# Two-block layer on one core: GpSimd's copy of the tokens moved behind the first product granule, and the rows of w_out split in the order of the features

## The chip, the cores and the metric

One Trainium2 chip, one core. The metric is the device time of one execution in microseconds, the median of several runs. The engines are TensorE (PE in the rows, PEld for its weight loads), VectorE (DVE), ScalarE (ACT), GpSimd (POOL) and SyncE (SP), which issues the DMAs.

## The reference, cut to what matters

256 tokens of 1024 features pass two blocks. The first is a hybrid mixer and then a mixture of 32 experts; the second is an LRU and gated-attention mixer and a dense feed-forward part. The change touches the entry and the end of the first mixer:

```
def first_block(x, ...):
    h = x
    hn = rmsnorm(h, norm_mix[i])
    h = h + hybrid_mixer(hn, w_in[i], ..., w_out[i])      # w_out: 2048 x 1024
    hn = rmsnorm(h, norm_ffn[i])
    h = h + hierarchical_moe(hn, ...)
    return rmsnorm(h, final_norm)

# the end of hybrid_mixer
    return jnp.concatenate([ssd_out, sc_out], axis=-1) @ w_out
```

`ssd_out` and `sc_out` are normed and carry a gain per feature (`ssd_norm`, `sc_norm`).

## The kernel before, in words

All matrices are fp32. A product is done in three fp32r passes: every weight is split into a high part (`w_hi`, rounded to fp32r) and the rest (`w_lo`), and so is every activation. Weights come in units of 2 MB, one of six slots of the buffer `ring` each; a unit is cut into four granules of 128 x 1024 elements. For granule g, ScalarE runs `hi(g)` (L583 without a gain, L585 with one), VectorE runs `lo(g)` (L593, or L595 with a gain), and TensorE multiplies. `w_hi` and `w_lo` hold two granules each, so `hi(g)` waits until TensorE has finished granule g-2 (it counts `gran_used`), `lo(g)` waits for `hi(g)`, and TensorE's granule g waits for both. Each engine's order is written out by hand, as one loop over g in which other steps are placed at fixed g.

**Opening.** The tokens land in `x_tok`. ScalarE squares block 0, VectorE block 1, GpSimd takes the power (L505). Then VectorE scales block 0 into `xdt` (L500) and ScalarE block 1 (L487); both are wanted by TensorE's 16 transposes (L515). `turn_act` and `turn_dve` (L534, L540) split the transposed tokens into `act_p`, and granule 0 follows (L613). From g = 2 on VectorE does one short convolution per granule behind `lo(g)` (`conv_xbc`, L1433, three steps with both inputs in SBUF). GpSimd, behind L505, copies `x_tok` to `res` (L912, two copies of 128 x 1024), makes two masks and `blk64` (L900 to L919), and then raises `const_ready` to 2. ScalarE waits for that before it overwrites `x_tok` (`keep_x(0)`, L1080, at g = 5).

**Order of features.** The residual `res` is kept in an order that makes later transposes give rows p of 8 features each: position c*128 + q of a row holds feature q*8 + c. `natural(b)` reads or writes `res` in the order of the features, which steps 128 elements (512 bytes) from one element to the next; `in_eights` of a bank has that order in one contiguous run.

**Output product.** `w_out` is units 11 to 14, granules 44 to 59 (G_WO = 44, GA = 60). Each of its granules is one row chunk of 128 x 1024, split with a gain (L585, L595), and TensorE adds 12 matmuls of 512 columns (`row_gran`, L664) to four banks. Behind the last granule `add_res` adds the four banks to `res` (L682), and TensorE transposes `res` for the router (L2200). The second block's mixer ends with `add_halves` (L691), where bank and `res` are both contiguous.

After the router come 32 experts, whose weights (6 MB each) stream from HBM.

Of the kernel before, what the change touches and what calls it, by code (L numbers as in the profile page):

```python
# [25 lines left out]
ALU = mybir.AluOpType  # L26
# [5 lines left out]
TB = T // P  # L32
D = 1024
KC = D // P
# [21 lines left out]
GR = 1024  # L56
# [19 lines left out]
def bcast(ap, shape):  # L76
    return ap.broadcast_to(shape)


def two_block_layer(nc, x, w, out):  # L80

    with ExitStack() as ctx:
        build(nc, ctx, x, w, out)


def build(nc, ctx, x, w, out):
    def sb(name, shape, dt=F32, where=ctx):
        return where.enter_context(nc.sbuf_tensor(name, shape, dt))

    def sem(name):  # L90
        return ctx.enter_context(nc.semaphore(name))
# [13 lines left out]
    res = sb("res", [P, TB, D])  # L105
# [25 lines left out]
    x_tok = sb("x_tok", [P, TB, D], where=ph)  # L131
# [60 lines left out]
    grans = []  # L192

    def whole(u):
        return ring[:, u % SLOTS, :]

    def cols_unit(wt, *spans):

        u = len(units)
        parts, at = [], 0  # L200
        for c0, n in spans:
            dst = whole(u).rearrange("p (k n) -> p k n", k=KC)[:, :, at:at + n]
            rows = "(p k) n -> p k n" if wt is w["w_in_2"] else "(k p) n -> p k n"
            parts.append((dst, wt.rearrange(rows, p=P)[:, :, c0:c0 + n]))
            at += n
        units.append(parts)
        return u

    def rows_unit(wt, chunk, n):

        u = len(units)
        dst = whole(u)[:, 0:n * D].rearrange("p (k n) -> p k n", k=n)
        src = wt[chunk * P:(chunk + n) * P, :].rearrange("(k p) n -> p k n", p=P)
        units.append([(dst, src)])
        return u
# [9 lines left out]
        for k in range(0, KC, kn):  # L225
            grans.append((u, whole(u).rearrange("p (k n) -> p k n", k=KC)[:, k:k + kn, c0:c0 + n], None))

    def row_grans(u, gains):
        for j, gain in enumerate(gains):
            grans.append((u, whole(u)[:, j * GR:(j + 1) * GR], gain))  # L230

    def sc_raw(c0, c1):

# [2 lines left out]
    def pcol(name, i):  # L236
        return par[:, PCOLS[name] + i:PCOLS[name] + i + 1]
# [12 lines left out]
    for c in range(0, 16, 4):  # L250
        ks = MIX[c:c + 4]
        row_grans(rows_unit(w["w_out"], ks[0], 4),
                  [pcol("sc_norm", k - 8) if k >= 8 else pcol("ssd_norm", k) for k in ks])
    UA, GA = len(units), len(grans)
    G_Q, G_K, G_V, G_G, G_LG = GA + 4, GA + 6, GA + 8, GA + 12, GA + 16
    turn_grans(cols_unit(w["w_in_2"], (0, P), (P, 512 - P)), range(4))
    u = cols_unit(w["w_in_2"], (O_Q, 512))
# [6 lines left out]
    for c in (0, 4):  # L264
        row_grans(rows_unit(w["w_out_2"], c, 4), [None] * 4)
# [10 lines left out]
    def ffn_out(f0, n):  # L276
        row_grans(rows_unit(w["w_ffn_out_2"], f0, n), [None] * n)
        for i in range(n):
            GO[f0 + i] = len(grans) - n + i
# [17 lines left out]
    const_ready = sem("const_ready")  # L297
# [3 lines left out]
    gran_used = sem("gran_used")  # L301
# [45 lines left out]
    ssd_norm = sem("ssd_norm")  # L347
# [92 lines left out]

    neg_half = sm[:, 8:24]
    N_ROWS_A = sum(tile == 0 for _, tile, _, _ in PROWS)
    N_SMALL = len(PROWS) + 3 + 2 + 1 + NG + 1 + 2 + 3

# [13 lines left out]
    def natural(b, p0=0, p1=P):  # L458

        return res[:, b, :].rearrange("t (c p) -> t p c", c=KC)[:, p0:p1, :]  # L460
# [8 lines left out]
    def in_eights(row):  # L469
        return row.rearrange("t (p c) -> t p c", c=KC)  # L470
# [32 lines left out]
    def norm_pool(pool, n):  # L503
        pool.wait_ge(ms_ready, n + 1)
        nc.gpsimd.tensor_tensor(sm[:, 4:6], sm[:, 2:4], neg_half[:, 0:2], ALU.pow).then_inc(rstd_ready, 1)  # L505
# [165 lines left out]
    def piece_ready(dve, n, at, g):  # L671
        if at < 3:
            dve.wait_ge(bank_done, 3 * n + at + 1)
        else:
            dve.wait_ge(gran_used, g + 1)

    def add_res(dve, n, g, banks, done):

        for at, (b, half) in enumerate(BY_BLOCK):
            r = natural(b, 64 * half, 64 * half + 64)  # L680
            piece_ready(dve, n, at, g)
            ins = nc.vector.tensor_tensor(r, r, in_eights(banks[2 * b + half][:, :]), ALU.add)  # L682
            if half:
                ins.then_inc(done, 1)

# [36 lines left out]
    for g, (u, _, _) in enumerate(grans):  # L722
        last_gran[u] = g
# [173 lines left out]
    def _(pool):  # L897
        def mask(tile, op, step, mult, base=0):
            plain = tile.bitcast(F32)
            link_pool(pool, nc.gpsimd.memset(plain, 1.0))  # L900
            link_pool(pool, nc.gpsimd.affine_select(out=tile, in_=plain, compare_op=op, fill=0.0, base=base,
                                                    pattern=[[step, P]], channel_multiplier=mult))
# [5 lines left out]
                       allow_small_or_imprecise_dtypes=True)  # L908
        nc.gpsimd.memset(pad[:, :, 0:3], 0.0).then_inc(const_ready, 1)
        norm_pool(pool, 0)  # L910
        for b in range(TB):
            nc.gpsimd.tensor_copy(natural(b), in_eights(x_tok[:, b, :]))  # L912
        mask(m_le[:, :], ALU.is_ge, 1, -1)
        mask(m_gt[:, :], ALU.is_gt, -1, 1)
        link_pool(pool, nc.gpsimd.memset(blk64[:, :], 1.0))
# [1 line left out]
        link_pool(pool, nc.gpsimd.affine_select(out=v, in_=v, compare_op=ALU.is_ge, fill=0.0, base=0,  # L917
                                                pattern=[[-64, 2], [0, 64]], channel_multiplier=1))
        nc.gpsimd.affine_select(out=v, in_=v, compare_op=ALU.is_ge, fill=0.0, base=63,  # L919
                                pattern=[[64, 2], [0, 64]], channel_multiplier=-1).then_inc(const_ready, 1)  # L920


        pool.wait_ge(u_ready, 1)
# [37 lines left out]
        def by_head(tile, b):  # L961
            return tile[:, b, :].rearrange("p (h d) -> p h d", h=HEADS)
# [21 lines left out]
        for b in range(TB):  # L984
            ins = nc.gpsimd.tensor_tensor(by_head(xdt, b), by_head(x_tok, b),
                                          bcast(adt[:, 7, b, :].unsqueeze(2), [P, HEADS, HD]), ALU.mult)
        ins.then_inc(xdt_ready, 1)
        for it in range(9):
# [16 lines left out]
            if it == 7:  # L1005
# [18 lines left out]
                                pattern=[[1, P]], channel_multiplier=-1).then_inc(const_ready, 1)  # L1024
# [376 lines left out]
    def _(dve):  # L1401
# [142 lines left out]
        for g in range(GA):  # L1544
# [32 lines left out]
            for h in range(2):  # L1577
                for n in range(2 * h, 2 * h + 2):
# [4 lines left out]
                    if g == (G_WO + 1, G_WO + 3)[h]:  # L1583
                        lo_ssd(n)
        add_res(dve, 0, GA - 1, bank[0:4], res_mix)


# [945 lines left out]
```

## Time and profile before

| | |
|---|---|
| median of 3 runs | 955.83 us (955.31 to 957.48) |
| the profiled execution's own time | 955.47 us |
| its span | 953.7 us |
| TensorE busy | 782.6 us, 82% |
| VectorE busy | 465.6 us, 49% |
| ScalarE busy | 318.0 us, 33% |
| GpSimd busy | 99.0 us, 10% |
| DMA | 286.67 MB, mean 301 GB/s |

The span is the time between the first and the last instruction that the trace shows; the execution's own time has 1.8 us around it. Busy times of engines overlap. The expert stage (about 240 to 640 us) runs with all 16 DMA engines busy; ahead of and behind it TensorE is the engine that is nearly always busy.

### The profile page before, as it was taken

The numbers are of one execution on the slowest core, as the hardware profiler recorded it, in microseconds if no ns is written. First come the engines' busy times: TensorE is split into PE (matmuls) and PEld (weight loads), VectorE is DVE, ScalarE is ACT, GpSimd is POOL, SyncE is SP. The second block draws the span as 40 slices with busy tenths as digits, with TensorE's granted clock in tenths as the row PEclk, the third lists the DMA queues.
The fourth block names the chain that finished last, engine by engine and source line by source line (L and its number), as shares of the span: only waits on it lengthen the run. The fifth ranks groups of instructions, "written<-read, shape, count | busy, mean of one in ns | idle before, by whom it ended". The sixth has DMA issues, their size and how long they took to land.

```text
span 953.7 us, 15749 instructions
## 1 busy us (share of the span) xinstructions
PE 782.6 (82%) x6548; PEld 601.2 (63%) x6548; DVE 465.6 (49%) x815; ACT 318.0 (33%) x525; POOL 99.0 (10%) x116
## 2 busy tenths in 40 slices
PE   5999999999984764747646566479999999999997
PEld 5988999777643432334423333236888888888885
DVE  6865849547421121201302012024968776766776
ACT  5764346732100000000000000003597554444444
POOL 3019673300000000000000000000000100000000
PEclk9999999999997887777979798779999999999999
DMA  9895243677999999999999999999975455555101
GB/s 318 272 354 177 90 177 145 259 311 294 415 427 428 426 429 426 427 427 429 428 429 427 428 429 427 429 428 388 363 266 178 155 189 201 183 177 177 45 1 45
DMA packets 72534, 286.67 MB, mean 301 GB/s; under 512 B 11882, under 2 KB 38688, under 8 KB 59936
## 3 DMA queue, kind: packets, MB, share of 16 engines
q1 hardware_dynamic: 71876, 284.81, 75.9%
q10 hardware_dynamic: 604, 1.10, 0.3%
q8 instruction: 39, 0.64, 0.3%
q14 instruction: 15, 0.12, 0.0%
HBM read 284.85 MB, written 1.05 MB: 300 GB/s over the span
## 4 chain that ended last, share of the span: by engine, by line
PE 54%; DMA 28%; issue 8%; DVE 4%; POOL 3%; ACT 2%; SPq 1%; POOLq 0%; DVEq 0%; ACTq 0%
DMA pair_d<-in_w_up_dram 22%; PE bank L664 11%; PE bank L613 11%; PE bank L629 9%; PE bank L2264 5%; PE bank L626 4%; PE bank L2288 4%; PE bank L641 4%; DMA ring<-in_w_in_dram 3%; DMA down_b<-in_w_down_dram 3%; PE bank L2230 1%; PE bank L2238 1%; PE bank L2095 1%; POOL seg_r L946 1%; ACT w_hi L583 1%
## 5 line engine op out<-in xcount | busy, mean ns | idle before, releaser
L593 DVE TENSOR_TENSOR w_lo<-ring,w_hi 128x1024 fp32r<-128x1024 f32 x135 | 174.7, 1294 | 101.9 <-ACT w_hi L583 101.5
L583 ACT ACTIVATE w_hi<-ring 128x1024 fp32r<-128x1024 f32 x136 | 144.2, 1060 | 178.3 <-PE bank L629 64.1
L613 PE MATMUL bank<-act_p,w_hi 128*128 128x256 f32 x736 | 137.7, 288 | 3.1 <-issue 2.0
L1776 DVE COPY y_e<-bank 32x256 f32<-32x256 f32 x64 | 27.2, 424 | 222.5 <-PE bank L2288 222.1
L629 PE MATMUL bank<-act_p,w_hi 128*128 128x512 f32 x344 | 119.3, 397 | 0.0
L613 PEld LDWEIGHTS bank<-act_p,w_hi 128*128 128x128 f32 x736 | 115.3, 192 | 6.0 <-issue 3.9
L1226 ACT ACTIVATE y_e<-bank 32x256 f32<-32x256 f32 x64 | 23.9, 374 | 256.7 <-PE bank L2288 256.4
L613 PE MATMUL bank<-act_p,w_lo 128*128 128x256 f32 x368 | 104.3, 283 | 0.0
L2288 PE MATMUL bank<-down_b,h_t 128*32 128x256 f32 x480 | 40.3, 493 | 74.6 <-issue 64.1
L664 PE MATMUL bank<-w_hi,act_q 128*128 128x512 f32 x288 | 90.6, 396 | 1.4 <-issue 0.8
L2264 PE MATMUL bank<-ring,moe 128*32 128x256 f32 x1472 | 84.0, 380 | 7.1 <-DVE moe L1739 6.7
L626 PE MATMUL bank<-act_p,w_lo 128*128 128x256 f32 x344 | 89.5, 281 | 0.0
L2288 PEld LDWEIGHTS bank<-down_b,h_t 128*32 128x32 f32 x480 | 18.9, 136 | 91.6 <-issue 74.0
L2264 PEld LDWEIGHTS bank<-ring,moe 128*32 128x32 f32 x1472 | 46.9, 110 | 38.6 <-issue 8.6
L629 PEld LDWEIGHTS bank<-act_p,w_hi 128*128 128x128 f32 x344 | 62.5, 188 | 13.1 <-issue 1.2
L613 PEld LDWEIGHTS bank<-act_p,w_lo 128*128 128x128 f32 x368 | 70.7, 192 | 0.0
L2264 PE MATMUL bank<-pair_d,moe 128*32 128x256 f32 x512 | 43.6, 515 | 30.4 <-DMA pair_d<-in_w_up_dram 30.4
L626 PEld LDWEIGHTS bank<-act_p,w_lo 128*128 128x128 f32 x344 | 64.9, 189 | 3.4
L664 PEld LDWEIGHTS bank<-w_hi,act_q 128*128 128x128 f32 x288 | 52.5, 188 | 15.0 <-issue 1.7
L2288 PE MATMUL bank<-down_a,h_t 128*32 128x256 f32 x480 | 37.9, 468 | 25.6 <-DMA down_a<-in_w_down_dram 25.6
L664 PE MATMUL bank<-w_lo,act_q 128*128 128x512 f32 x144 | 56.3, 391 | 0.0
L2264 PEld LDWEIGHTS bank<-pair_d,moe 128*32 128x32 f32 x512 | 24.3, 146 | 49.5 <-issue 46.1
(409 smaller groups left out, 1058.5 us busy)
## 6 DMA issues: line engine op xcount, KB each, us to landing
ring<-in_w_up_dram SPq DMA_DIRECT2D x24, 2048.0 KB, 34.6
ring<-in_w_gate_dram SPq DMA_DIRECT2D x23, 2048.0 KB, 30.2
down_a<-in_w_down_dram SPq DMA_DIRECT2D x15, 2048.0 KB, 25.9
down_b<-in_w_down_dram SPq DMA_DIRECT2D x15, 2048.0 KB, 25.8
ring<-in_w_in_dram SPq DMA_DIRECT2D x14, 2048.0 KB, 17.4
ring<-in_w_ffn_in_dram SPq DMA_DIRECT2D x22, 1024.0 KB, 7.6
pair_d<-in_w_gate_dram SPq DMA_DIRECT2D x8, 2048.0 KB, 30.0
pair_d<-in_w_up_dram SPq DMA_DIRECT2D x8, 2048.0 KB, 34.4
```

The lines of the kernel that those rows point to most:

```text
L583: nc.scalar.activation(parts(w_hi, g, view), view, ACT.Copy).then_inc(split_hi, 1)
L593: engine.tensor_tensor(parts(w_lo, g, view), view, h, ALU.subtract).then_inc(split_lo, 1)
L613: mm = nc.tensor.matmul(dst, parts(wt, g, grans[g][1])[:, k, :], a[:, x_part, k, :], start=(k == 0 and i == 0), stop=(k == KC - 1 and i == 2))
L626: mm = nc.tensor.matmul(dst[:, 0:T], parts(w_lo, g, grans[g][1])[:, k, :], a[:, 0, k, :], start=False, stop=False)
L629: mm = nc.tensor.matmul(dst[:, :], parts(w_hi, g, grans[g][1])[:, k, :], a[:, :, k, :], start=(k == 0), stop=(k == KC - 1))
L641: mm = nc.tensor.matmul(dsts[b], a[:, x_part, k0 + k, b * P:(b + 1) * P], parts(wt, g, grans[g][1])[:, k, :], start=(k0 + k == 0 and i == ...
L664: mm = nc.tensor.matmul(banks[2 * b + half][:, :], a_chunk[:, x_part, b * P:(b + 1) * P], wt[:, slot(g), half * 512:(half + 1) * 512], sta ...
L946: ins = nc.gpsimd.tensor_tensor(seg_r[:, n, :, :], bcast(m_le[:, :].unsqueeze(1), [P, 4, P]), bcast(adt_r[:, n, b, 4 * q:4 * q + 4].bitcas ...
L1226: ins = nc.scalar.activation(out_rows(e, j), down_rows(j), ACT.Copy)
L1776: ins = nc.vector.tensor_copy(out_rows(e, j), down_rows(j))
L2264: mm = nc.tensor.matmul(bank[GU_BANK[e % 2]][CAP * j:CAP * (j + 1), 0:2 * P], x_t[:, c, CAP * e:CAP * (e + 1)], gu[:, :, c, j * P:(j + 1) ...
L2288: mm = nc.tensor.matmul(bank[2][CAP * j:CAP * (j + 1), 0:256], h_t[:, e % 2, CAP * c:CAP * (c + 1)], dn[:, c, 256 * j:256 * (j + 1)], star ...
```

## The change

Three edits.

1. GpSimd's two copies of `x_tok` to `res` are moved from ahead of the masks to behind them, and wait until TensorE has finished granule 0 (`gran_used` at 1). The last increment of `const_ready` moves to the second copy.
2. The granules of `w_out` are read from `ring` through a view that takes every eighth element (32 bytes from one to the next), so that `w_hi` and `w_lo` hold their columns in the order of `res`.
3. The banks therefore come out in the order of `res`, and `add_res` reads and writes `res` contiguously.

```diff
-    def row_grans(u, gains):
+    def row_grans(u, gains, eights=False):
         for j, gain in enumerate(gains):
-            grans.append((u, whole(u)[:, j * GR:(j + 1) * GR], gain))
+            view = whole(u)[:, j * GR:(j + 1) * GR]
+            grans.append((u, view.rearrange("p (q c) -> p c q", c=KC) if eights else view, gain))
...
         row_grans(rows_unit(w["w_out"], ks[0], 4),
-                  [pcol("sc_norm", k - 8) if k >= 8 else pcol("ssd_norm", k) for k in ks])
+                  [pcol("sc_norm", k - 8) if k >= 8 else pcol("ssd_norm", k) for k in ks], True)
...
         for at, (b, half) in enumerate(BY_BLOCK):
-            r = natural(b, 64 * half, 64 * half + 64)
+            r = res[:, b, half * 512:(half + 1) * 512]
             piece_ready(dve, n, at, g)
-            ins = nc.vector.tensor_tensor(r, r, in_eights(banks[2 * b + half][:, :]), ALU.add)
+            ins = nc.vector.tensor_tensor(r, r, banks[2 * b + half][:, :], ALU.add)
...
         norm_pool(pool, 0)
-        for b in range(TB):
-            nc.gpsimd.tensor_copy(natural(b), in_eights(x_tok[:, b, :]))
         mask(m_le[:, :], ALU.is_ge, 1, -1)
         mask(m_gt[:, :], ALU.is_gt, -1, 1)
...
         nc.gpsimd.affine_select(out=v, in_=v, compare_op=ALU.is_ge, fill=0.0, base=63,
-                                pattern=[[64, 2], [0, 64]], channel_multiplier=-1).then_inc(const_ready, 1)
+                                pattern=[[64, 2], [0, 64]], channel_multiplier=-1)
+        pool.wait_ge(gran_used, 1)
+        for b in range(TB):
+            ins = nc.gpsimd.tensor_copy(natural(b), in_eights(x_tok[:, b, :]))
+        ins.then_inc(const_ready, 1)
```

GpSimd's queue in the opening, before. L505 is the power of the norm, L912 the copies, L900 and L901 the masks, L915 to L919 `blk64`, L695 the first step of the softplus at about 66 us.

```order
14 L505 TENSOR_TENSOR sm<-sm 128x2 [waits ms_ready]
15 L912 COPY res<-x_tok 128x128x8 x2
16 L900 MEMSET m_le 128x128
17 L901 AFFINE_SELECT m_le<-m_le 128x128 [waits pool_chain]
18 L900 MEMSET m_gt 128x128 [waits pool_chain]
19 L901 AFFINE_SELECT m_gt<-m_gt 128x128 [waits pool_chain]
20 L915 MEMSET blk 128x128 [waits pool_chain]
21 L917 AFFINE_SELECT blk<-blk 128x128 [waits pool_chain]
22 L919 AFFINE_SELECT blk<-blk 128x128 [waits pool_chain]
23 L695 TENSOR_TENSOR adt<-adt 128x32 [waits u_ready]
```

The same stretch of GpSimd's queue with the change (its lines are numbered one to ten higher):

```order
14 L506 TENSOR_TENSOR sm<-sm 128x2 [waits ms_ready]
15 L901 MEMSET m_le 128x128
16 L902 AFFINE_SELECT m_le<-m_le 128x128 [waits pool_chain]
17 L901 MEMSET m_gt 128x128 [waits pool_chain]
18 L902 AFFINE_SELECT m_gt<-m_gt 128x128 [waits pool_chain]
19 L914 MEMSET blk 128x128 [waits pool_chain]
20 L916 AFFINE_SELECT blk<-blk 128x128 [waits pool_chain]
21 L918 AFFINE_SELECT blk<-blk 128x128 [waits pool_chain]
22 L922 COPY res<-x_tok 128x128x8 [waits gran_used]
23 L922 COPY res<-x_tok 128x128x8
24 L696 TENSOR_TENSOR adt<-adt 128x32 [waits u_ready]
```

The two copies stand last of the opening, behind a wait for TensorE; nothing else in this queue moved. The orders of the other engines are the same; in VectorE's the adds of the output product change their form, from 128x64x8 before

```order
148 L682 TENSOR_TENSOR res<-res,bank 128x64x8 [waits bank_done] x3
149 L682 TENSOR_TENSOR res<-res,bank 128x64x8 [waits gran_used]
```

to one run of 512 with the change:

```order
148 L683 TENSOR_TENSOR res<-res,bank 128x512 [waits bank_done] x3
149 L683 TENSOR_TENSOR res<-res,bank 128x512 [waits gran_used]
```

## Rows read from the trace of the kernel before

**Rows 1.** The page's chain that ended last, by line.

```profile
DMA pair_d<-in_w_up_dram 22%; PE bank L664 11%; PE bank L613 11%; PE bank L629 9%; PE bank L2264 5%; PE bank L626 4%; PE bank L2288 4%; PE bank L641 4%; DMA ring<-in_w_in_dram 3%; DMA down_b<-in_w_down_dram 3%; PE bank L2230 1%; PE bank L2238 1%; PE bank L2095 1%; POOL seg_r L946 1%; ACT w_hi L583 1%
```

**Rows 2.** The chain in order of time, 0 to 75 us: start, us, what.

```profile
8.27 2.45 DVE xdt L500
...
14.50 12.21 PE bank L613 x96
...
30.21 2.88 PE bank L613 x24
```

**Rows 3.** GpSimd's timeline, opening: start us, us, engine, line, operation, tiles, forms.

```profile
8.20 4.34 POOL L912 COPY res<-x_tok 128x1024 f32<-128x1024 f32 x2
12.39 0.26 POOL L900 MEMSET m_le<- 128x128 f32 x1
...
14.94 0.29 POOL L919 TENSOR_SCALAR_AFFINE_SELECT blk<-blk 128x128 f32<-128x128 f32 x1
```

**Rows 4.** The instructions of line 912: duration ns min/median/max, first and last start.

```profile
L912 POOL COPY res<-x_tok x2: 1964/2241/2518, 8.2 to 10.0; 128x1024 f32<-128x1024 f32 x2
```

**Rows 5.** ScalarE's timeline, opening.

```profile
8.27 1.15 ACT L487 ACTIVATE xdt<-x_tok,sm 128x1024 f32<-128x1024 f32 x1 [1.24 <-POOL sm L505]
...
18.17 1.06 ACT L583 ACTIVATE w_hi<-ring 128x1024 fp32r<-128x1024 f32 x1 [2.21 <-PE bank L613]
```

**Rows 6.** VectorE's timeline, opening.

```profile
10.79 2.67 DVE L593 TENSOR_TENSOR w_lo<-ring,w_hi 128x1024 fp32r<-128x1024 f32 x1
...
19.33 1.23 DVE L593 TENSOR_TENSOR w_lo<-ring,w_hi 128x1024 fp32r<-128x1024 f32 x1 [1.61 <-ACT w_hi L583]
20.47 1.52 DVE L1433 SCALAR_TENSOR_TENSOR cv<-pad,par,cv 128x256 f32<-128x256 f32 x3
22.08 1.23 DVE L593 TENSOR_TENSOR w_lo<-ring,w_hi 128x1024 fp32r<-128x1024 f32 x1
```

**Rows 7.** Groups by line and form, VectorE: busy us, mean ns | idle before.

```profile
L682 DVE TENSOR_TENSOR res<-res,bank 128x512 f32<-128x512 f32 x4 | 4.0, 1056 | 1.1 <-PE bank L664 1.1
L691 DVE TENSOR_TENSOR res<-res,bank 128x512 f32<-128x512 f32 x4 | 2.7, 688 | 1.1 <-PE bank L664 1.1
...
L1820 DVE TENSOR_TENSOR nrm<-res,down_c 128x1024 f32<-128x1024 f32 x2 | 4.0, 2044 | 0.0
...
L1906 DVE TENSOR_TENSOR lpad<-lpad,lx 128x1024 f32<-128x1024 f32 x1 | 1.2, 1219 | 0.0
...
L1776 DVE COPY y_e<-bank 32x256 f32<-32x256 f32 x64 | 27.2, 424 | 222.5 <-PE bank L2288 222.1
```

**Rows 8.** Groups by line and form, ScalarE.

```profile
L585 ACT ACTIVATE w_hi<-ring,par 128x1024 fp32r<-128x1024 f32 x16 | 18.4, 1149 | 17.4 <-PE bank L664 17.4
L1226 ACT ACTIVATE y_e<-bank 32x256 f32<-32x256 f32 x64 | 23.9, 374 | 256.7 <-PE bank L2288 256.4
L1066 ACT ACTIVATE pad<-bank 128x256 f32<-128x256 f32 x12 | 4.4, 366 | 0.0
```

**Rows 9.** The chain in order of time, output product.

```profile
187.70 17.08 PE bank L664 x72
```

**Rows 10.** ScalarE's timeline, output product.

```profile
181.74 1.15 ACT L585 ACTIVATE w_hi<-ring,par 128x1024 fp32r<-128x1024 f32 x1
...
185.17 1.15 ACT L585 ACTIVATE w_hi<-ring,par 128x1024 fp32r<-128x1024 f32 x1
...
202.16 1.15 ACT L585 ACTIVATE w_hi<-ring,par 128x1024 fp32r<-128x1024 f32 x1 [1.81 <-PE bank L664]
```

**Rows 11.** VectorE's timeline, output product.

```profile
203.42 1.28 DVE L595 SCALAR_TENSOR_TENSOR w_lo<-ring,par,w_hi 128x1024 fp32r<-128x1024 f32 x1 [1.74 <-ACT w_hi L585]
```

**Rows 12.** TensorE's timeline, output product.

```profile
204.80 0.70 PE L664 MATMUL bank<-w_hi,act_q 128*128 128x512 f32 x2
```

**Rows 13.** Stretches: length, busy of PE, PEld, DVE, ACT, POOL, then PEclk, DMA share, GB/s.

```profile
228.00:234.00 6.00, 6.00 (x59) 5.00 (x62) 3.77 (x18) 0.00 (x0) 0.00 (x0) 1.00 0.28 117
...
300.00:600.00 300.00, 179.97 (x2130) 102.92 (x2130) 55.08 (x150) 20.50 (x60) 0.00 (x0) 0.82 1.01 428
```

## The prediction

> **What bounds the kernel now.** I read the chain that ended last, by line [rows 1], then in order of time [rows 2, 9], then the timelines of the three engines that take part at the opening and at the output product, and last the stretches with their DMA share. The chain is TensorE's work (PE) wherever the change acts: from 14.50 us on the products of L613 stand in it without a gap for 12.21 us [rows 2], and in the output product 72 matmuls of L664 in 17.08 us [rows 9]. That is 2.85 us for the 12 matmuls of a granule. Behind the router the chain is a stream of expert weights: from 300 to 600 us the DMA share is 1.01 [rows 13]. Is a microsecond won or lost ahead of that stream lost in it? From 228 to 234 us the DMA share is 0.28 [rows 13], so its queue ran empty and waited for the products of the first experts. The saturated stretch starts when these are done; whatever moves the end of the output product moves the end of the program by as much.
>
> **Opening, the part that gains.** GpSimd's first copy starts at 8.20 [rows 3]. VectorE's scaling L500 starts at 8.27 and takes 2.45 us [rows 2]. The two copies take 1.96 and 2.52 us [rows 4]: the first ends at about 10.0, and L500 at 10.72; the second, which was to start at 10.0, ends at 12.54. The split that starts at 10.79 takes 2.67 us [rows 6], where the same form takes 1.23. All of that fits one picture: a copy and such a VectorE instruction exclude each other for a whole instruction, and a copy alone takes 12.54 - 10.72 = 1.8 us. With the copies gone from here, L500 should end before ScalarE's L487, at 9.42 [rows 5], and the transposes, which need both, start 10.72 - 9.42 = **1.3 us** earlier. The masks that move up (2.8 us, from 12.39 to 15.23 [rows 3]) run while VectorE waits; were they to hold L500 by one memset of 0.26, it would still end ahead of 9.42.
>
> **Opening, the part that gives back.** The copies now wait for granule 0. ScalarE's split of granule 2 waits for the same event and starts at 18.17 [rows 5], 16.9 with the gain. Copy 1 runs from 16.9 to 18.7. VectorE's split of granule 2 is due at 19.33 - 1.3 = 18.0 [rows 6] and waits to 18.7; it ends at 19.9. Copy 2 has stood in line since 18.7, so it goes next, to 21.7. The convolution behind the split (20.47 before [rows 6]) reads two inputs from SBUF and waits until 21.7, and the split of granule 3 follows 22.08 - 20.47 = 1.6 later, at 23.3, and ends at 24.5. TensorE started that granule at 26.71 - 2.88 = 23.8 before [rows 2]. So it starts at 24.6, **0.8 us late**; from there TensorE has no gap in which to make it up. What is queued behind GpSimd's wait costs nothing: its next work starts at about 66 us, and ScalarE wants `const_ready` only at g = 5. Bounds: 1.3 gained if the copies cost VectorE nothing here; 2.1 lost if the gain does not show.
>
> **Adds.** An add takes 1056 ns with `res` at 512-byte steps (L682) and 688 ns contiguous (L691) [rows 7]: 0.37 each, 1.5 us for four. TensorE releases them one by one, 2.85/4 = 0.71 apart, which is more than 0.69. The four then take 3 x 0.71 + 0.69 = 2.8 instead of 4.0 [rows 7]: 1.2. Block 0's transposes stand between, so I take **1.0 us gained**; bounds 0.8 and 1.5.
>
> **Splits of w_out.** Sixteen of ScalarE's and sixteen of VectorE's now read `ring` in 32-byte steps. No row shows that read. Nearest on VectorE is L1820: one of its two SBUF inputs steps 512 bytes, and it takes 2044 ns where L1906 of the same size, all contiguous, takes 1219 [rows 7]: 0.82 for 1024 elements. Reads of a bank in 32-byte steps cost nothing, on VectorE (L1776: 424 ns [rows 7]) nor on ScalarE (L1226: 374 ns for 256 elements, contiguous L1066 366 [rows 8]); since VectorE shows both at once, free from a bank and dear from SBUF, the bank rows say little of `ring`. I take 0.82 for VectorE, and, with the same memory behind it, 0.82 for ScalarE too. Bounds: nothing, and twice 0.82 on VectorE if short steps are worse than long ones.
>
> Is there room for it? Granule g's split on ScalarE waits for TensorE to finish g-2. From 202.16 [rows 10]: 1.15, then VectorE from 203.42 to 204.70 [rows 11], TensorE from 204.80 [rows 12], 2.85 for the granule, about 0.2 until ScalarE starts again: 2.64 + 2.85 + 0.2 = 5.7 us for a pair, and 2 x 2.85 is 5.7. There is none. Each pair of granules is longer by the sum of what both splits gain in length, 1.64. That holds for the nine granules 51 to 59: 9 x 0.82 = 7.4. Ahead of them, granule 45 waits for one split of each engine: 1.64. Then ScalarE's splits of granules 48 to 50 stand in one chain with logarithms and exponentials between (181.74 to 185.17 for one step [rows 10]): 3 x 0.82, and 0.82 for VectorE's last. Together 4.9. **12.3 us lost.**
>
> The Trainium skill (Vector Engine (DVE) Microarchitecture Reference, section 5.2) says that a VectorE port keeps its full rate only in runs of at least two adjacent 4-byte words, and that a short fixed step, 24 words, took 2.50 ns per element against 1.73 for long hops. Estimated from that page, a split could take 2.6 us and the sum would be near 971; no row here shows a short step.
>
> **Sum.** 955.47 (the profiled execution; its span is 953.7, and the median of the runs is 0.36 above it) + 0.8 - 1.0 + 12.3 = **967.5 us**.
>
> **Rivals.**
> - *ScalarE reads the steps for free* and only VectorE pays. For it: the bank rows. Against: they do not cost VectorE anything either. Granule 45 and 50 lose 0.82 each, nine more 0.41: 5.3. Time 955.47 + 0.8 - 1.0 + 5.3 = 960.6. Chance 0.25.
> - *Faster: a 32-byte step is as free from SBUF as from a bank*, on both engines. Place: the loop of 5.7 us; it decides as soon as both splits together grow by less than some 0.1. Then the adds' 1.0 stays, and the opening decides how far: 955.3 with its loss of 0.8, 953.2 if the copies hide and its 1.3 stays. For it: again the bank rows. Against: L1820 and L682. Chance 0.15, of which 0.09 for the faster end.
> - *Short steps cost VectorE twice as much*, 1.64. Granule 45: 2.46; the chain of three and one: 2.46 + 1.64; nine at 1.23: 11.1. Sum 17.7, time 972.9. Chance 0.12.
> - *The copies cost nothing behind granule 0*: VectorE's splits do not wait for them. Against: the 2.67. It takes 2.1 off any case: 965.4 for the forecast. I hold it inside each case.
>
> **How the numbers follow.** The forecast has 0.45 and the rivals 0.25, 0.15 and 0.12; 0.03 is for what I do not see. The range goes from 958.5 (the first rival with 2.1 off) to 973 (the third). Below 958.5 lies the faster rival, above little. Some 0.2% (1.9 us) is what a measurement of this kernel can tell from no change. Faster by more: 0.09. Within: 0.11 (the rest of that rival, and prices well under 0.82). Slower: 0.80.
>
> **What would show it.** In the opening: L500 at 0.8 to 1.1 us, transposes from 9.6, two copies from about 16.9, the second with VectorE's split waiting or ahead of it, granule 3 at 24.6. In the output product: ScalarE's w_out split near 1.97 instead of 1.15, VectorE's near 2.1, granules 3.6 to 3.7 us apart on average instead of 2.85, with TensorE waiting for `w_lo`. The adds at 0.69. From 256 us on, the same times as before, shifted by one amount. I am wrong if the splits keep their 1.15 and 1.28, if granules stay 2.85 apart in spite of longer splits, or if the shift at 256 us is not the one at the end.

## The result, and the profile after

| | before | after |
|---|---|---|
| median, us | 956.22 (4 runs, 955.31 to 957.48) | 971.98 (4 runs, 970.72 to 973.38) |
| the profiled execution, us | 955.47 | 970.72 |
| its span, us | 953.7 | 969.0 |
| VectorE busy, us | 465.6 | 476.5 |
| ScalarE busy, us | 318.0 | 335.8 |

The ratio is 1.0164 (95% interval 1.0142 to 1.0187): slower by 15.8 us. The forecast was 967.5 us, within 958.5 to 973.

**Where the time went.** The page's chain by line, after:

```profile
DMA pair_d<-in_w_up_dram 21%; PE bank L614 11%; PE bank L665 10%; PE bank L630 9%; PE bank L2267 4%; PE bank L627 4%; PE bank L2291 4%; PE bank L642 3%; DMA ring<-in_w_in_dram 3%; DMA down_b<-in_w_down_dram 3%; ACT w_hi L586 2%; DVE w_lo L596 2%; PE bank L2233 1%; PE bank L2241 1%; PE bank L2098 1%
```

Against [rows 1] two entries are new, ScalarE's and VectorE's splits of `w_out` (L586, L596, 2% each). They were hidden behind TensorE before and are now on the path. L614, L665 and L630 are before's L613, L664 and L629.

The same chain in order of time, before, at the places where the two can be laid side by side (start us, us, what; lines that also stand in [rows 9] are not repeated):

```profile
93.24 5.81 PE bank L613 x48
...
112.33 3.10 PE bank L613 x24
116.74 5.83 PE bank L613 x48
...
214.12 3.97 DVE res L682 x4
...
219.22 3.51 PE bank L2209 x32
...
230.08 3.49 PE bank L2238 x32
...
256.54 31.92 DMA pair_d<-in_w_up_dram
```

And after:

```profile
93.58 5.81 PE bank L614 x48
...
112.65 4.30 PE bank L614 x24
...
118.57 5.81 PE bank L614 x48
...
195.24 3.03 PE bank L665 x12
...
233.88 3.73 PE bank L2212 x32
237.61 4.96 PE bank L2043 x8
...
245.40 3.49 PE bank L2241 x32
...
271.86 31.91 DMA pair_d<-in_w_up_dram
```

VectorE's timeline has the adds, which replaced the row 214.12:

```profile
229.96 2.77 DVE L683 TENSOR_TENSOR res<-res,bank 128x512 f32<-128x512 f32 x4 [1.07 <-PE bank L665]
```

The delay of after against before at each of these places gives a budget that needs no model:

| from, to | delay at the end | of it here | predicted |
|---|---|---|---|
| opening, to 93 us | 93.58 - 93.24 = 0.34 | +0.34 | +0.8 |
| the granule at 112 us | 118.57 - 116.74 = 1.83 | +1.5 | none |
| output product, to the first add | 229.96 - 214.12 = 15.84 | +14.0 | +12.3 |
| adds, to L2212 (L2209) | 233.88 - 219.22 = 14.66 | -1.2 | -1.0 |
| router, to L2241 (L2238) | 245.40 - 230.08 = 15.32 | +0.66 | none |
| start of the stream of weights | 271.86 - 256.54 = 15.32 | 0 | 0 |
| end | 970.72 - 955.47 = 15.25 | -0.1 | 0 |

**The output product.** The splits by form (busy us, mean ns | idle before), after:

```profile
L596 DVE SCALAR_TENSOR_TENSOR w_lo<-ring,par,w_hi 128x1024 fp32r<-128x1024 f32 x16 | 35.2, 2198 | 21.5 <-ACT w_hi L586 21.5
...
L683 DVE TENSOR_TENSOR res<-res,bank 128x512 f32<-128x512 f32 x4 | 2.7, 687 | 1.1 <-PE bank L665 1.1
...
L586 ACT ACTIVATE w_hi<-ring,par 128x1024 fp32r<-128x1024 f32 x16 | 36.5, 2284 | 14.2 <-PE bank L665 14.2
```

ScalarE's went from 1149 ns [rows 8] to 2284, by **1.135 us**. VectorE's went from a mean of 1328 ns (most single ones are at the 1.28 us of [rows 11]) to a mean of 2198, with a median of 2156: **0.87 us** more. The chain in order of time shows the loop that this makes:

```profile
206.17 3.03 PE bank L665 x12
...
209.22 2.26 ACT w_hi L586
...
211.50 2.25 DVE w_lo L596
...
213.79 3.05 PE bank L665 x12
```

Every step waits for the one before it: TensorE's granule, ScalarE's split into the part of `w_hi` that this granule set free, VectorE's split, and TensorE's granule two further on. A round takes 213.79 - 206.17 = 7.6 us, the next two starts are at 221.34 and 228.94, where the 72 matmuls of before, 17.08 us in one piece [rows 9], are 5.7 us for two granules. TensorE's timeline shows what it waits for, once per round:

```profile
210.48 0.74 PE L665 MATMUL bank<-w_hi,act_p 128*128 128x512 f32 x2 [1.30 <-DVE w_lo L596]
```

**The opening.** VectorE's timeline, after:

```profile
8.36 0.75 DVE L501 TENSOR_SCALAR xdt<-x_tok,sm 128x1024 f32<-128x1024 f32 x1 [0.83 <-POOL sm L506]
...
18.34 1.78 DVE L594 TENSOR_TENSOR w_lo<-ring,w_hi 128x1024 fp32r<-128x1024 f32 x1 [1.55 <-ACT w_hi L584]
20.05 3.15 DVE L1436 SCALAR_TENSOR_TENSOR cv<-pad,par,cv 128x256 f32<-128x256 f32 x3
```

and GpSimd's:

```profile
17.15 4.90 POOL L922 COPY res<-x_tok 128x1024 f32<-128x1024 f32 x2 [6.27 <-PE bank L614]
```

The scaling takes 0.75 us instead of 2.45 [rows 2]. In return, the split of granule 2 takes 1.78 instead of 1.23, and the convolution behind it 3.15 instead of 1.52 [rows 6]: both run into the copies. What is left of both is in the chain:

```profile
3.30 5.99 DMA seg_e<-in_ssd_norm_dram
...
9.34 0.44 PE bank L2048
9.78 3.46 PE bank L516 x16
...
24.38 3.15 PE bank L614 x24
```

Granule 3 starts at 24.38 instead of 23.8. The chain gives L516 only from 9.78, where the modelled end of the matmul ahead of it (L2048) lies, which waits for a small DMA that lands at 9.3. TensorE's timeline has the start of the transposes itself at 9.57 instead of 10.86, right behind ScalarE's scaling, which ends at 8.36 + 1.15 = 9.51. So the DMA did not hold them.

**Two stretches at a lower clock.** The granted clock is the clock that TensorE was given, as a share of its full speed. Stretches of after: length, busy of PE, PEld, DVE, ACT, POOL, then granted clock, DMA share, GB/s:

```profile
107.00:119.00 12.00, 10.20 (x71) 9.82 (x70) 9.84 (x15) 3.98 (x6) 5.27 (x5) 0.86 0.27 111
...
237.60:242.50 4.90, 4.90 (x11) 2.15 (x10) 4.32 (x24) 0.00 (x0) 0.00 (x0) 0.72 1.00 428
```

The first stretch before:

```profile
107.00:119.00 12.00, 10.18 (x83) 9.87 (x82) 11.36 (x17) 3.65 (x6) 6.84 (x6) 1.00 0.25 102
```

0.86 is a mean over TensorE's two levels, 2.4 and 1.2 GHz: part of the stretch was at the lower one, and the same 24 matmuls took 4.30 us instead of 3.10. In the second stretch eight matmuls that only keep TensorE running while VectorE works for the router (L2043, `keep_running`) stand in the chain for 4.96 us; before, the granted clock was 1.00 here and the chain went through VectorE. No step of the prediction speaks of it; the experiments say whether the change brings it.

### The profile page after: what moved, and what is told of

Read it like the earlier page. It is cut to its first block, busy times and chain, and to the rows that moved or that the text cites. A ratio compares the mean times of both kernels' runs of the same rounds, so it can differ in the third digit from the quotient of the medians.

```text
span 969.0 us, 15749 instructions
## 1 busy us (share of the span) xinstructions
PE 788.2 (81%) x6548; PEld 603.9 (62%) x6548; DVE 476.5 (49%) x815; ACT 335.8 (35%) x525; POOL 100.4 (10%) x116
## 4 chain that ended last, share of the span: by engine, by line
PE 54%; DMA 27%; issue 8%; DVE 4%; ACT 3%; POOL 2%; SPq 1%; ACTq 0%; POOLq 0%; DVEq 0%
DMA pair_d<-in_w_up_dram 21%; PE bank L614 11%; PE bank L665 10%; PE bank L630 9%; PE bank L2267 4%; PE bank L627 4%; PE bank L2291 4%; PE bank L642 3%; DMA ring<-in_w_in_dram 3%; DMA down_b<-in_w_down_dram 3%; ACT w_hi L586 2%; DVE w_lo L596 2%; PE bank L2233 1%; PE bank L2241 1%; PE bank L2098 1%
## 5 line engine op out<-in xcount | busy, mean ns | idle before, releaser
L614 PE MATMUL bank<-act_p,w_hi 128*128 128x256 f32 x736 | 139.2, 290 | 4.1 <-DVE w_lo L594 2.1
L614 PEld LDWEIGHTS bank<-act_p,w_hi 128*128 128x128 f32 x736 | 116.2, 194 | 7.3 <-issue 3.5
L630 PE MATMUL bank<-act_p,w_hi 128*128 128x512 f32 x344 | 119.3, 398 | 0.0
L614 PE MATMUL bank<-act_p,w_lo 128*128 128x256 f32 x368 | 105.0, 285 | 0.0
L665 PE MATMUL bank<-w_hi,act_q 128*128 128x512 f32 x288 | 90.5, 395 | 5.8 <-DVE w_lo L596 3.3
L614 PEld LDWEIGHTS bank<-act_p,w_lo 128*128 128x128 f32 x368 | 71.3, 194 | 0.0
L630 PEld LDWEIGHTS bank<-act_p,w_hi 128*128 128x128 f32 x344 | 62.7, 188 | 13.1 <-issue 1.2
L665 PEld LDWEIGHTS bank<-w_hi,act_q 128*128 128x128 f32 x288 | 52.3, 188 | 20.3 <-DVE w_lo L596 5.7
L1224 ACT ACTIVATE h_e<-bank 128x128 f32<-128x128 f32 x32 | 8.9, 277 | 137.0 <-PE bank L2267 136.3
L665 PE MATMUL bank<-w_lo,act_q 128*128 128x512 f32 x144 | 56.3, 391 | 0.0
```

The lines of the kernel that those rows point to most:

```text
L614: mm = nc.tensor.matmul(dst, parts(wt, g, grans[g][1])[:, k, :], a[:, x_part, k, :], start=(k == 0 and i == 0), stop=(k == KC - 1 and i == 2))
L630: mm = nc.tensor.matmul(dst[:, :], parts(w_hi, g, grans[g][1])[:, k, :], a[:, :, k, :], start=(k == 0), stop=(k == KC - 1))
L665: mm = nc.tensor.matmul(banks[2 * b + half][:, :], a_chunk[:, x_part, b * P:(b + 1) * P], wt[:, slot(g), half * 512:(half + 1) * 512], sta ...
```

## The experiments

Two theories. **One**: reading `ring` in 32-byte steps makes both splits longer, the loop adds the two, and the opening and the adds are small. **Two** (the rival): the moved copies are a good part of the loss, by delaying VectorE and by what follows (the slow granule at 112 us). A side question was whether the adds' gain and the opening's gain can be had without their prices. Kernels of one group ran on one chip, beside the kernel before.

### The opening move alone

```diff
 # before
-        for b in range(TB):
-            nc.gpsimd.tensor_copy(natural(b), in_eights(x_tok[:, b, :]))
...
+        pool.wait_ge(gran_used, 1)
+        for b in range(TB):
+            ins = nc.gpsimd.tensor_copy(natural(b), in_eights(x_tok[:, b, :]))
+        ins.then_inc(const_ready, 1)
```

> Only GpSimd's two copies are moved behind granule 0; w_out and the adds are as before. Theory 1 (splits pay for the loss, the move nearly nothing): transposes start about 1.1 us earlier, TensorE's granule 3 about 0.7 later, end +0.6 us, so 956.0 to 957.0. Theory 2 (the moved copies also cause the slower matmuls seen at 112 to 118 us of the changed kernel): end +2 us or more, 958. Either way w_out's splits keep 1.15 and 1.28 us.

Measured: 957.26 us (11 runs) against 957.02 (24 runs), ratio 1.0004 [0.9995, 1.0013]. The chain's opening of this kernel:

```profile
17.84 1.79 DVE w_lo L593
19.64 2.05 DVE cv L1435
...
23.91 3.15 PE bank L613 x24
```

Granule 3 starts at 23.91, 0.1 later than before. So the move is worth nothing either way that can be measured: what is won ahead of granule 0 is lost again behind it. Its chain has the slow granule too, 4.60 us at 112 us:

```profile
112.49 4.60 PE bank L613 x24
```

but its median is that of before. Theory two falls for the copies themselves.

### The split order alone

```diff
 # the changed kernel
+        for b in range(TB):
+            nc.gpsimd.tensor_copy(natural(b), in_eights(x_tok[:, b, :]))
...
-        pool.wait_ge(gran_used, 1)
-        for b in range(TB):
-            ins = nc.gpsimd.tensor_copy(natural(b), in_eights(x_tok[:, b, :]))
-        ins.then_inc(const_ready, 1)
```

> Only w_out's splits read in 32-byte steps and the adds are contiguous; GpSimd copies at the old place. Theory 1: ScalarE's split 2.2 to 2.35 us, VectorE's 2.1 to 2.2, end of the output product +14, adds -1.2, end +13 us: 968.5 to 970. Theory 2: the move had 2 us or more of the loss, so this one is at 968 or below.

Measured: 970.62 us (4 runs), ratio 1.0137 [1.012, 1.0155]: 13.6 us. ScalarE's split takes 2271 ns here, VectorE's 2203, an add 687. Nearly the whole loss comes with the order. The stretch from 107 to 119 us is at a mean clock of 0.86 here too, with the copies at their old place.

### One engine's reads contiguous

The price of each engine's split, and the arithmetic of the loop, by giving one of the two its contiguous read back. The base is the kernel with the split order alone. In the first kernel ScalarE reads and writes contiguously while VectorE steps; `w_hi` then holds another weight's high part at each position; `w_lo` is taken against it, so their sum is still the weight, and the expectation's words on the value go too far: only the pass of `w_hi` with the activations' low part changes.

```diff
 # ScalarE contiguous
-            nc.scalar.activation(parts(w_hi, g, view), view, ACT.Copy, scale=gain).then_inc(split_hi, 1)
+            flat = whole(u)[:, (g - G_WO) % 4 * GR:((g - G_WO) % 4 + 1) * GR]
+            nc.scalar.activation(w_hi[:, slot(g), :], flat, ACT.Copy, scale=gain).then_inc(split_hi, 1)
```

> As order_only, but ScalarE's split of w_out reads contiguously (1.15 us) and only VectorE's reads in 32-byte steps; w_hi and w_lo then belong to different columns, so the output product's value is another one. Loop theory (a pair of granules lasts ScalarE's split + VectorE's split + one granule): VectorE's +0.83 costs 2 x 0.83 once and 0.42 for each of nine granules, 5.4, less 1.2 of the adds: +4.2 us, 961. Rival (VectorE's split alone is long enough to bind): nearly the whole +13, 969.

Measured: 961.91 us (4 runs) against 955.74 (15 runs), ratio 1.0061 [1.0046, 1.0076]: 6.2 us. The splits by form:

```profile
L597 DVE SCALAR_TENSOR_TENSOR w_lo<-ring,par,w_hi 128x1024 fp32r<-128x1024 f32 x16 | 35.5, 2219 | 11.6 <-ACT w_hi L587 11.6
L587 ACT ACTIVATE w_hi<-ring,par 128x1024 fp32r<-128x1024 f32 x16 | 18.4, 1149 | 22.1 <-PE bank L666 22.1
```

And a round of the chain:

```profile
209.66 1.16 ACT w_hi L587
210.85 2.18 DVE w_lo L597
213.07 3.03 PE bank L666 x12
```

The round is 6.5 us: 5.7 and VectorE's 0.8 to 0.9. The time grew by 6.2 where 4.2 was expected. By the chain the loop itself did as expected (3.9 for 3.8); 0.65 more came ahead of granule 50, 0.2 in the opening, and 0.7 in the router, where this kernel's trace has the stretch at the lower clock too (5.21 us, as in the changed kernel's 4.96).

```diff
 # VectorE contiguous, ScalarE in steps
-            nc.vector.scalar_tensor_tensor(out=parts(w_lo, g, view), in0=view, scalar=gain, in1=h,
+            flat = whole(u)[:, (g - G_WO) % 4 * GR:((g - G_WO) % 4 + 1) * GR]
+            nc.vector.scalar_tensor_tensor(out=w_lo[:, slot(g), :], in0=flat, scalar=gain, in1=w_hi[:, slot(g), :].bitcast(F32),
```

> As order_only, but VectorE's split of w_out reads contiguously and only ScalarE's (2.28 us) reads in steps; the output product's value is another one. Loop theory: ScalarE's +1.13 counts four times at the start (granule 45, and 48 to 50 in its own chain) and 0.57 for each of nine granules, 9.6, less 1.2: +8.4 us, 965.5. The two parts together 14.9 less 1.2, about what both gave (13.6).

Measured: 963.56 us (4 runs), ratio 1.0078 [1.0062, 1.0093]: 7.8 us. A round of its chain:

```profile
209.60 2.25 ACT w_hi L586
211.94 1.29 DVE w_lo L597
213.33 3.00 PE bank L666 x12
```

The round is 6.8 us: 5.7 and ScalarE's 1.1. In time it is 7.8 for 8.4 expected. Both kernels keep the adds' gain of 1.2, so without that gain VectorE's steps cost 7.4 and ScalarE's 9.0, together 16.4 where both at once cost 13.6 + 1.2 = 14.8. The difference of 1.6 lies within the three intervals, each some 1.5 us to either side. The rounds say it more sharply: 0.8 and 1.1 alone, 1.9 (7.6 - 5.7) together. So the two prices add, as one loop has it. That ScalarE's is the larger is read from the lengths and the rounds; the intervals of the two times overlap.

### The step moved to TensorE's read

If the step has to be somewhere, TensorE could take it: splits contiguous, and the moving operand of L664 read in 32-byte steps, so that the banks still come out in the order of `res`.

```diff
 # the split order alone, with contiguous splits
-                                      wt[:, slot(g), half * 512:(half + 1) * 512],
+                rhs = wt[:, slot(g), half * 512:(half + 1) * 512]
+                if g < GA:
+                    rhs = wt[:, slot(g), :].rearrange("p (q c) -> p c q", c=KC)[:, 4 * half:4 * half + 4, :]
```

> The splits are contiguous as before; TensorE reads w_hi and w_lo of w_out in 32-byte steps instead, and the adds are contiguous. If a step costs TensorE nothing, a matmul of 512 columns keeps its 0.23 us pitch and the end is -1.2 us, 955.5. If each element is a fetch of its own, as the splits suggest (0.8 ns more for an element), a matmul takes 0.41 more, 192 of them 79 us: above 1030.

Measured: 991.52 us (4 runs), ratio 1.037 [1.0354, 1.0386]: 35.8 us slower. Chain in order of time:

```profile
172.07 5.17 PE bank L667 x12
```

Twelve matmuls take 5.2 us instead of 2.85. Neither value of the expectation came: the step makes a matmul of 512 columns 1.8 times as long, 0.43 instead of 0.24 us. 16 x 2.35 is 37.6, less the adds' 1.2 makes 36.4. It is the dearest of the three places.

### The step moved to the bank

The adds can have a contiguous `res` with the splits left alone: half h of a bank holds features 512h to 512h + 511, which are 64 positions of each of the eight runs of `res`, so the bank is read in 32-byte steps and `res` in runs of 64.

```diff
 # before
-            r = natural(b, 64 * half, 64 * half + 64)
+            r = res[:, b, :].rearrange("t (c p) -> t c p", c=KC)[:, :, 64 * half:64 * half + 64]
-            ins = nc.vector.tensor_tensor(r, r, in_eights(banks[2 * b + half][:, :]), ALU.add)
+            ins = nc.vector.tensor_tensor(r, r, banks[2 * b + half][:, :].rearrange("t (p c) -> t c p", c=KC), ALU.add)
```

> The kernel before with one line changed: the adds walk res in its own order (runs of 64 elements) and read the bank in 32-byte steps; w_out is split as before. If a step of 32 bytes is free from a bank on VectorE also with a second input from SBUF, an add takes 0.69 to 0.72 us, the adds end 1.2 us earlier, end -1.0 us: 954.8. If the bank's steps cost what SBUF's did, adds stay at 1.05 and the time does not move.

Measured: 955.25 us (12 runs) against 957.02, ratio 0.9987 [0.9975, 0.9999]. By form:

```profile
L682 DVE TENSOR_TENSOR res<-res,bank 128x512 f32<-128x512 f32 x4 | 2.7, 688 | 1.1 <-PE bank L664 1.1
```

688 ns, the time of the contiguous L691 [rows 7]. This is edit 3's whole gain of 1.2 us without edit 2.

### Without the copies

How much can the placing of the copies bring at most? The adds from the bank in steps, and no copies at all.

```diff
 # the adds with the step in the bank
+        nc.gpsimd.memset(res[:, :, :], 0.0)
-        for b in range(TB):
-            nc.gpsimd.tensor_copy(natural(b), in_eights(x_tok[:, b, :]))
```

> As the kernel with the adds that read the bank in steps, but GpSimd's two copies are left out: res is set to zero in an idle stretch ahead (the residual x is missing from the output). The lower bound of the opening: if the placed copies hide fully, this equals placed, 953.7; if they still cost something, it is below it by that. The copies' price at their old place is the difference to psum_adds, 1.1 us by the traces.

Measured: 954.2 us (11 runs), ratio 0.9981 [0.9972, 0.999], against 955.74. That is 1.5 us, of which the adds are 1.2; the 0.3 that is left for the copies cannot be told from nothing. The trace says more: the granule at 111 us starts 1.27 us earlier than before (111.06 against 112.33), so the placing has about 1.3 to give. This kernel has neither the order of the splits nor the copies, and yet its chain holds both slow pieces of after, which take that gain away again in this execution:

```profile
111.06 4.35 PE bank L613 x24
...
221.62 5.21 PE bank L2039 x8
```

It was expected at or below the next kernel, where the copies are placed; by the ratios (0.9981 and 0.9971) it is not below it.

### The copies where VectorE waits

Copy 0 may start once VectorE's scaling is done (`nrm_dve`), copy 1 once its split of granule 0 is done (`split_lo`); in both gaps VectorE waits for others, or runs `turn_dve`, which has one input from a bank.

```diff
 # the adds with the step in the bank
-        for b in range(TB):
-            nc.gpsimd.tensor_copy(natural(b), in_eights(x_tok[:, b, :]))
+        pool.wait_ge(nrm_dve, 1)
+        nc.gpsimd.tensor_copy(natural(0), in_eights(x_tok[:, 0, :]))
+        pool.wait_ge(split_lo, 1)
+        nc.gpsimd.tensor_copy(natural(1), in_eights(x_tok[:, 1, :]))
```

> As the kernel with the adds that read the bank in steps, and GpSimd's copies placed where VectorE reads at most one SBUF tensor: copy of block 0 when VectorE's scaling is done, copy of block 1 when split 0 is done (beside turn_dve, which reads a bank and one SBUF tensor). Theory 1 (exclusion only against instructions with two SBUF inputs or VectorE's two-port copies): no VectorE instruction gets longer, TensorE's granule 3 starts 1.1 us earlier than before, end -2.1 us: 953.7. Rival (GpSimd's copy slows turn_dve too): turn_dve longer than 3.3 us and the opening gains under 0.5.

Measured: 953.73 us (6 runs), ratio 0.9971 [0.9959, 0.9982]. The same kernel again, on another chip:

> placed once more, beside placed_open and the kernel before on one chip: 2.4 us below the kernel before (1.2 of the opening, 1.2 of the adds), ratio 0.9975. Rival: the first ratio of 0.9971 was the chip's scatter, 0.999 or above.

953.44 us (6 runs) against 957.0 (17 runs), ratio 0.9963 [0.995, 0.9975]. The opening on the two engines in this second run, GpSimd:

```profile
9.30 2.01 POOL L912 COPY res<-x_tok 128x1024 f32<-128x1024 f32 x1 [0.85 <-DVE xdt L500]
12.29 2.03 POOL L914 COPY res<-x_tok 128x1024 f32<-128x1024 f32 x1 [0.98 <-DVE w_lo L593]
```

and VectorE:

```profile
12.14 3.22 DVE L540 SCALAR_TENSOR_TENSOR act_p<-bank,par,act_p 128x256 fp32r<-128x256 f32 x8
...
18.18 1.22 DVE L593 TENSOR_TENSOR w_lo<-ring,w_hi 128x1024 fp32r<-128x1024 f32 x1 [1.68 <-ACT w_hi L583]
19.33 1.52 DVE L1435 SCALAR_TENSOR_TENSOR cv<-pad,par,cv 128x256 f32<-128x256 f32 x3
```

No instruction is stretched: splits at 1.23, the convolution at 1.52, copies at 2.0 each. The chain:

```profile
13.35 12.21 PE bank L613 x96
...
92.10 5.81 PE bank L613 x48
```

Granule 0 starts 1.15 us earlier than before [rows 2], and that head start is still there at 92 us (93.24 before). With the adds' 1.2 this kernel beats the kernel before by 0.3 to 0.4%, and with it the changed one. The medians give 3.3 and 3.6 us, the traces account for 2.4 (254.19 instead of 256.54 us at the start of the stream); 2.4 lies in the first interval and at the edge of the second. The placing alone, with the adds as before:

> Only the opening of placed: GpSimd's two copies beside instructions of VectorE that read at most one SBUF tensor; adds and w_out as in the kernel before. If the two gains are separate, TensorE is 1.1 to 1.3 us ahead from granule 3 to the end of the output product and the time is 1.2 us below the kernel before. Rival: the head start is lost again on the way (a wait on GpSimd's later chain or on a landing), no difference.

955.79 us (12 runs), ratio 0.9994 [0.9982, 1.0006]. Its trace has the head start too (91.76 instead of 93.24 us, and 254.93 instead of 256.54 at the start of the stream), but its timing does not tell it from no change. So the pair of edits is shown to be faster, the adds alone just so, the placing alone is not.

## Why the prediction was right or wrong

**Right by its own steps.** What bounds the kernel was read rightly: the delay at the start of the weight stream (15.32) is the delay at the end (15.25). The adds gained 1.2 where 1.0 was predicted, 687 ns each. The loop was the decisive step: "There is none" (no room), and every pair of granules longer by what both splits gain. Measured: pairs of 7.6 us, 5.7 + 1.135 + 0.87 = 7.7. The loop alone (from 195.24 to the first add, against 187.70) lost (229.96 - 195.24) - (214.12 - 187.70) = 8.3, the piece ahead of it 5.7 (7.54 less the 1.83 that was there already); 7.4 and 4.9 were predicted.

**How near, and by what luck.** The forecast was 12.0 us over the profiled execution before; the profiled execution after is 15.25 over it. Of the 3.2 between them 2.2 are the two stretches at a lower clock, which the prediction did not have. The rest is 1.7 too little for the output product against 0.5 too much loss in the opening and 0.2 too little gain from the adds. The median, 971.98, lies 1 us inside the upper bound, and that bound was set for a rival that did not come true (VectorE's price doubled). That the number fell within the range is in part luck; the loop and where the time went are not.

**The term that was mis-sized.** "I take 0.82 for VectorE, and, with the same memory behind it, 0.82 for ScalarE too." VectorE's 0.87 was near. ScalarE's was 1.135, and the same memory does not make the same price. With 1.135 and 0.87 the prediction's own sum would be 9 x 1.0 = 9.0 in the loop and 2.0 + 3 x 1.135 + 0.87 = 6.3 ahead of it, 15.3, where 8.3 and 5.7 were measured. So its shape counts some 1.3 us too much: 0.7 in the rounds (1.9 each instead of 2.0, and 8.3 in all), and 0.6 ahead of them, where granule 45 lost 1.2 and not 2.0 (it starts at 173.88 instead of 170.89 on TensorE's timeline, less the 1.83). This hid a part of the price that it had too low.

**The opening.** Right in kind, a little off in size. Predicted: transposes from 9.6, granule 3 at 24.6, 0.8 late. Measured: 9.57 and 24.38, 0.6 late. The order of the two engines' work came out as predicted: copy 1 holds VectorE's split (to 20.12, predicted 19.9), the split goes ahead of copy 2, and copy 2 holds the first step of the convolution (2.04 in the chain, where the other two take 0.5). A copy alone takes 2.0 us (2.01 and 2.03 in the kernel that places them apart), not the 1.8 that was worked out. Of the delay 0.34 is left at 93 us. It is 0.62 at 70.87 us, and the rest goes by 77.6 us in GpSimd's chain of decays. Its small operations take 0.25 to 0.3 us, or 1.1 to 1.3 where a split of VectorE runs beside them (before: 1.32 at 72.19, beside the split at 72.17). After, the same operation ran at 72.81 in 0.25, just ahead of the split at 72.83, and the next one was held instead, for 1.14. No step of the prediction had this.

**Not foreseen.** 1.5 us at 112 us and 0.66 in the router, both at a lower granted clock. The first belongs to no one edit. The twelve profiles (one kernel was profiled twice) show the granule at 112 us either at 3.1 us or at 4.3 to 4.6: slow in five, the changed kernel and those with the move alone, with the split order alone, with VectorE contiguous and without copies; fast in before and in the six others, among them the one with ScalarE contiguous. The kernel with the move alone shows it and has before's median. The matmuls that keep TensorE running in the router stand in the chain for 4.96 to 5.21 us in five profiles, the changed kernel and those with the split order alone, with ScalarE contiguous, without copies and with the copies placed. The last of these, profiled a second time, does not have it: here the same kernel goes both ways. The three profiles with the slow adds never have it; whether the shorter adds make it likelier is open. So the profiled execution of after carries 1.5 and 0.66 us that the comparison of medians need not; without both stretches the budget is 0.34 + 14.0 - 1.2 = 13.1 us, and the medians say 15.8 for the whole change and 13.6 for the order alone. The 2 us between these are no larger than the two intervals (each about 1.7 to 2.2 us to either side), and stay open. The four runs of after are 970.72 and 970.80 at a mean granted clock of 0.923, and 973.17 and 973.38 at 0.918 and 0.920; their median lies in the gap.

**The rivals.** That ScalarE reads the steps for free: refuted, its price is the larger. That they are free altogether: refuted. That a short step costs VectorE twice 0.82: refuted, 0.87. The Trainium skill's 2.50 ns per element for a short step (Vector Engine (DVE) Microarchitecture Reference, section 5.2) was measured with both sources, or the destination alone, in that step; a 32-byte step on one source does not give it here: 2156 ns (the median) for 1024 elements is 2.1 ns each, between the page's long hops and its short step. That estimate, near 971, came closer to the measured time than the forecast did, but with the extra price on the wrong engine. That the copies cost nothing behind granule 0: refuted, the split and the convolution were stretched by 0.55 and 1.6.

## What to carry to other kernels

A change of order between two buffers has a step somewhere, and what counts is where: here it was free in a read of a bank (688 ns), 0.37 us per 512 elements in `res`, 0.87 to 1.14 us per 1024 in a split's read of SBUF, and 1.8 times the time in TensorE's moving operand. Put it where the elements are fewest and the memory is the accumulation bank, not into the weights, of which there were 16 granules for four adds. Before lengthening a step that the profile shows with idle time around it (ScalarE had 17.4 us before L585), add up the loop that it stands in: that idle time was the other members' time.

When a copy on GpSimd has to share the opening with VectorE, start it by the event after which VectorE waits for others, and not by one that also starts VectorE's next work. The gain of this is 1.2 us in the traces; in time it is shown only together with the adds'.

## What the runs showed of the hardware

- A 32-byte step in an fp32 read of SBUF costs ScalarE more than VectorE: 1149 to 2284 ns against 1328 to 2198 (means) for 128 x 1024. The same step from a bank costs neither anything (688 ns for VectorE's add; L1226 in [rows 8] for ScalarE).
- The same step in the moving operand takes 12 matmuls of 512 columns from 2.85 to 5.2 us.
- GpSimd's copy and a VectorE instruction that reads two inputs from SBUF hold each other up, and so do the copy and the scaling L500, which has one input and takes 0.75 us for 1024 elements when alone; `turn_dve`, with one of its inputs from a bank, ran beside the copy at its 3.22 us. A GpSimd operation of 0.25 us took 1.32 beside a split of VectorE. The Trainium skill has this as an exclusive lock on a shared pair of ports (SBUF — State Buffer, "Who interferes with whom"), and the runs agree both ways: 1.78 for a split and 3.15 for the convolution beside a copy, 1.23 and 1.52 without.
- The granted clock falls in the same place, around 112 us, in some profiled executions of nearly the same program and not in others, and costs 1.2 to 1.5 us. It falls during the granule behind a wait in which TensorE is nearly idle (busy for 0.2 of 2.0 us); that wait is there in both kinds. Nothing that the engines did in the 20 us ahead of it tells the two kinds apart; why stays open. In the router the same kernel has such a stretch in one execution (0.68 over 5.2 us) and not in another.
